# Seven-product pairs of the FFN up-projection in groups of two with one ordinary pair between, and their fourth weight sum made by VectorE instead of an adding DMA

## The reference, cut to what matters

```python
D_FF = 2816
def conv_ffn(x, w_up, conv_w, conv_b, w_down):
    h = x @ w_up                       # (512, 1024) @ (1024, 5632)
    ch = h.shape[-1]
    h = lax.conv_general_dilated(h, conv_w[:, None, :], window_strides=(1,), padding=((CONV_WIDTH - 1, 0),), ...,
                                 feature_group_count=ch) + conv_b
    gate, val = jnp.split(h, 2, axis=-1)
    return (jax.nn.silu(gate) * val) @ w_down
```

## Time and profile before

| | us |
|---|---|
| median of three runs | 2041.09 |
| the profiled execution's own time | 2042.29 |
| its span, first to last instruction | 2040.6 |
| PE busy | 2026.4 (99%) |
| DVE (VectorE) busy | 1619.3 (79%) |
| ACT (ScalarE) busy | 1115.0 (55%) |
| POOL (GpSimd) busy | 433.7 (21%) |

### The profile page before, as it was taken

One profiled execution on the slowest core, in us unless ns is written; L12 is line 12 of the kernel. 1 busy time (PEld: TensorE's weight loads), 2 busy tenths in 40 slices (PEclk: granted clock), 3 DMA queues, 4 the chain that ended last, 5 costly groups with the idle time before them and its releaser, 6 DMA issues.

```text
span 2040.6 us, 33333 instructions
## 1 busy us (share of the span) xinstructions
PE 2026.4 (99%) x12636; PEld 1750.7 (86%) x12636; DVE 1619.3 (79%) x2555; ACT 1115.0 (55%) x1861; POOL 433.7 (21%) x482
## 2 busy tenths in 40 slices
PE   9999999999999999999999999999999999999998
PEld 8889998888988899888877888998888889999887
DVE  6668878889467887899888669777997668877898
ACT  4755545447335555546656646555465755545555
POOL 0520332210000232120035402322110520332220
PEclk9999999999999999999999999999999999999999
DMA  8123344384432334467421123334674122334393
GB/s 291 64 104 125 109 130 150 121 255 172 145 129 75 97 105 129 145 190 243 166 73 42 63 83 104 119 104 155 197 237 163 65 104 83 109 122 147 115 269 122
DMA packets 82570, 276.42 MB, mean 135 GB/s; under 512 B 9408, under 2 KB 13632, under 8 KB 82032
## 3 DMA queue, kind: packets, MB, share of 16 engines
q1 hardware_dynamic: 59184, 214.67, 30.4%
q0 software_dynamic: 11200, 24.12, 5.8%
q10 hardware_dynamic: 12032, 35.54, 4.8%
HBM read 256.43 MB, written 14.73 MB: 133 GB/s over the span
## 4 chain that ended last, share of the span: by engine, by line
PE 91%; DVE 5%; DMA 2%; ACT 1%; issue 0%; DVEq 0%; ACTq 0%; SPq 0%
PE ps L2437 12%; PE ps L2438 12%; PE ps L2439 12%; PE ps L2649 6%; PE ps L3018 5%; PE ps L3019 5%; PE ps L3020 5%; PE ps L2976 5%; PE ps L2978 5%; PE ps L2977 5%; PE ps L2509 2%; PE ps L2465 2%; PE ps L2466 2%; PE ps L2467 2%; DMA raw<-slabs 2%; PE ps L2497 1%
## 5 line engine op out<-in xcount | busy, mean ns | idle before, releaser
L2437 PE MATMUL ps<-h_hi,w_hi 128*128 128x512 f32 (+1 forms) x1104 | 433.0, 392 | 0.0
L2438 PE MATMUL ps<-h_lo,w_hi 128*128 128x512 f32 (+1 forms) x1104 | 429.6, 389 | 0.0
L2439 PE MATMUL ps<-h_hi,w_lo 128*128 128x512 f32 (+1 forms) x1104 | 428.9, 389 | 0.0
L1603 DVE TENSOR_TENSOR w_lo<-raw,w_hi 128x1024 fp32r<-128x1024 f32 x300 | 372.0, 1247 | 39.1 <-ACT w_hi L901 35.5
L901 ACT ACTIVATE w_hi<-raw 128x1024 fp32r<-128x1024 f32 x312 | 326.4, 1053 | 133.1 <-DVE raw L2251 74.0
L2437 PEld LDWEIGHTS ps<-h_hi,w_hi 128*128 128x128 f32 x1104 | 207.6, 188 | 44.0 <-issue 4.0
L2439 PEld LDWEIGHTS ps<-h_hi,w_lo 128*128 128x128 f32 x1104 | 207.3, 188 | 43.2
L2438 PEld LDWEIGHTS ps<-h_lo,w_hi 128*128 128x128 f32 x1104 | 207.7, 188 | 38.9
L1281 ACT ACTIVATE work<-ps,conv_sb 128x512 f32<-128x512 f32 x120 | 93.0, 775 | 162.6 <-PE ps L2439 133.2
L3018 PE MATMUL ps<-w_hi,h_hi 128*128 128x512 f32 x408 | 159.7, 391 | 2.1 <-DVE w_lo L1603 2.1
L3020 PE MATMUL ps<-w_hi,h_lo 128*128 128x512 f32 x408 | 158.8, 389 | 0.0
(11 more groups left out here) (365 smaller groups left out, 5054.6 us busy)
## 6 DMA issues: line engine op xcount, KB each, us to landing
raw<-slabs SPq DMA_DIRECT2D x368, 512.0 KB, 4.1
act<-slabs POOLq DMA_DIRECT2D x64, 256.0 KB, 5.6
bias<-slabs SPq DMA_DIRECT2D x16, 512.0 KB, 6.3
x_dram<-x ACTq DMA_DIRECT2D x16, 512.0 KB, 5.0
x<-x_dram ACTq DMA_DIRECT2D x16, 512.0 KB, 4.9
raw<-act POOLq DMA_DIRECT2D x28, 256.0 KB, 3.3
act<-slabs SPq DMA_DIRECT2D x12, 512.0 KB, 5.4
bias_dram<-bias_rows ACTq DMA_DIRECT2D x2, 2048.0 KB, 12.3
```

What stands on the lines that cost most here:

```text
L1603: ve.tensor_tensor(w_lo[:, c % RING, :], raw[:, raw_slot(c), :], w_hi[:, c % RING, :].bitcast(f32), ALU.subtract).then_inc(lo_made, 1)
L2437: pe.matmul(ps[:, bank, cols], hi, h_hi[:, k, cols], start=k == 0, stop=False)
L2438: pe.matmul(ps[:, bank, cols], hi, h_lo[:, k, cols], start=False, stop=False)
L2439: last = pe.matmul(ps[:, bank, cols], lo, h_hi[:, k, cols], start=False, stop=k == KT - 1)
```

## The change

The seven-product pairs become 4, 6, 7, 9, 10, 12, 13, 15 and 16, nine in a layer in place of seven. Pair 4 with pair 5 keeps a queue of its own (`first_period`), and four groups follow, of two seven-product pairs f and g = f + 1 and one ordinary pair n = f + 2 (f = 6, 9, 12, 15). PSUM's eight banks go round in fours of two for all pairs of this stretch. In a group TensorE runs p1, p2, p6, p5, p7 of f, p1 and p2 of g, p4 and p3 of f, p6, p5, p7 of g, the first slab of n, p4 and p3 of g, the second slab of n. The fourth weight sum is made by VectorE (`x4`) and the adding DMA is gone. SP's loads stand in the order of the pairs. Both engines' queues are written anew. Cut to its core:

```diff
-FASTS = (FAST_END - FAST) // 2
+GROUPS_OF_THREE = 6, 9, 12, 15
+FAST_PAIRS = [FAST] + [q + e for q in GROUPS_OF_THREE for e in range(2)]
+FASTS = len(FAST_PAIRS)
+X1_ORDER = [FAST] + [q + e for q in GROUPS_OF_THREE for e in (1, 0)]
+UP_PRODUCTS = [(FAST, p) for p in (1, 2, 6, 4, 3)] + [
+    (q + e, p) for q in GROUPS_OF_THREE
+    for e, p in ((0, 1), (0, 2), (0, 6), (1, 1), (1, 2), (0, 4), (0, 3), (1, 6), (1, 4), (1, 3))]
...
-            return (0 if q // 2 % 2 else 4) + e
+            return 2 * ((q + 2) % 4 if FAST <= q < FAST_END else q % 2) + e
...
-                for q in range(FAST, FAST_END + 2, 2):
+                for q in range(FAST, FAST_END + 1):
                     for e in range(2):
                         c = up_slab(L, q, e)
-                        if q == FAST:
+                        if q - 2 not in FAST_PAIRS:
                             sp.wait_ge(lo_made, made(c - RAW))
                         elif e:
-                            sp.wait_ge(part_lo_made["x3"], fast(L, q - 2) + 1)
-                            sp.wait_ge(part_lo_made["x4"], fast(L, q - 2) + 1)
+                            sp.wait_ge(part_lo_made["x3"], part_count(L, q - 2, "x3"))
+                            sp.wait_ge(part_lo_made["x4"], part_count(L, q - 2, "x4"))
                         else:
-                            sp.wait_ge(part_lo_made["x1"], fast(L, q - 2) + 1)
+                            sp.wait_ge(part_lo_made["x1"], part_count(L, q - 2, "x1"))
                             sp.wait_ge(up_x2, fast(L, q - 2) + 1)
                             sp.wait_ge(up_x3, fast(L, q - 2) + 1)
                         sp.dma_start(raw[:, raw_slot(c), :], slabs[dram(c)]).then_inc(raw_in[raw_slot(c)], 16)
-                    if q < FAST_END:
-                        for e in range(2):
-                            c = up_slab(L, q + 1, e)
-                            sp.wait_ge(lo_made, made(c - RAW))
-                            sp.dma_start(raw[:, raw_slot(c), :], slabs[dram(c)]).then_inc(raw_in[raw_slot(c)], 16)
...
-            def fourth_sum(L, q):
-                pool.wait_ge(up_x2, fast(L, q) + 1)
-                pool.wait_ge(part_lo_made["a11"], fast(L, q) + 1)
-                pool.dma_start(raw[:, raw_slot(up_slab(L, q, 1)), SEQ:D], sum_place(), accum_op=ALU.add)\
-                    .then_inc(up_x4, 16)
...
-                fourth_sum(L, FAST)
                 for j in range(STEPS - 1):
                     down_sums(L, j)
-                    if FAST <= 2 * j + 4 < FAST_END and j:
-                        fourth_sum(L, 2 * j + 4)
...
+                def period(f):
+                    g, n = f + 1, f + 2
+                    more = n + 1 < FAST_END
+                    slab_tap(f - 1, 1)
+                    part_hi(f, "x3")
+                    copy(f, 0)
+                    part_hi(g, "a11")
+                    slab_silu(f - 1)
+                    copy(f, 1)
+                    part_hi(f, "x4")
+                    copy(f, 2)
+                    part_hi(g, "x2")
+                    copy(g, 0)
+                    part_hi(g, "x3")
+                    slab_tap(f, 0)
+                    split_hi(up_slab(L, n))
+                    slab_tap(f, 1)
+                    copy(g, 1)
+                    slab_silu(f)
+                    split_hi(up_slab(L, n, 1))
+                    part_hi(g, "x4")
+                    copy(g, 2)
+                    if more:
+                        part_hi(f + 4, "x1")
+                        slab_tap(g, 0)
+                        part_hi(f + 3, "a11")
+                        part_hi(f + 3, "x2")
+                        slab_tap(g, 1)
+                        part_hi(f + 3, "x1")
                     else:
                         sc.dma_start(x[:, 0, :], x_dram[0]).then_inc(x_back, 16)
                         sc.dma_start(x[:, 1, :], x_dram[1]).then_inc(x_back, 16)
                         operand(L, 0)
                         for j in range(4):
                             s1(L, j)
-                        fast_tap(q, 0)
+                        slab_tap(g, 0)
                         sc.dma_start(x[:, 2, :], x_dram[2]).then_inc(x_back, 16)
                         sc.dma_start(x[:, 3, :], x_dram[3]).then_inc(x_back, 16)
-                        sc.wait_ge(up_mm, 5 * fast(L, q) + 5)
-                        split_hi(up_slab(L, q + 2))
-                        fast_tap(q, 1)
-                        split_hi(up_slab(L, q + 2, 1))
-                    silu(0, i)
-                    tap(1, i, 0)
+                        split_hi(up_slab(L, n + 1))
+                        slab_tap(g, 1)
+                        split_hi(up_slab(L, n + 1, 1))
+                    slab_tap(n, 0)
+                    slab_silu(g)
...
+                def x4(q):
+                    row1 = raw_slot(up_slab(L, q, 1))
+                    ve.wait_ge(up_x2, fast(L, q) + 1)
+                    ve.wait_ge(part_lo_made["a11"], part_count(L, q, "a11"))
+                    ve.tensor_tensor(raw[:, row1, SEQ:D], raw[:, row1, SEQ:D], sum_place(), ALU.add).then_inc(up_x4, 1)
...
                 def x2(q):
@@ -2084,7 +2147,8 @@
                     ve.wait_ge(raw_in[row1], raw_count(up_slab(L, q, 1)))
                     if q > FAST:
                         ve.wait_ge(part_lo_made["x2"], fast(L, q))
-                        ve.wait_ge(up_x4, 16 * fast(L, q))
+                        ve.wait_ge(up_x3, fast(L, q))
+                        ve.wait_ge(up_x4, fast(L, q))
...
+                def first_period(q):
                     slab_taps(q - 1, 1)
-                    if q > FAST:
-                        part_lo(q, "x3")
                     split_lo(up_slab(L, q + 1))
-                    gate(1, i - 1)
+                    slab_gate(q - 1)
                     split_lo(up_slab(L, q + 1, 1))
                     c11(q)
                     part_lo(q, "x4")
                     c22(q)
-                    if q + 2 < FAST_END:
-                        x1(q + 2)
-                        x2(q + 2)
-                        part_lo(q + 2, "a11")
-                        part_lo(q + 2, "x2")
-                        slab_taps(q, 0)
-                        c12(q)
-                        part_lo(q + 2, "x1")
-                        slab_taps(q, 1)
-                        x3(q + 2)
+                    x1(q + 2)
+                    x2(q + 2)
+                    x1(q + 3)
+                    part_lo(q + 2, "a11")
+                    part_lo(q + 2, "x2")
+                    slab_taps(q, 0)
+                    c12(q)
+                    part_lo(q + 3, "x1")
+                    part_lo(q + 2, "x1")
+                    slab_taps(q, 1)
+                    x3(q + 2)
+                    slab_gate(q)
+                    x4(q + 2)
...
+                def period(f):
+                    g, n = f + 1, f + 2
+                    more = n + 1 < FAST_END
+                    slab_tap(f - 1, 0, 1)
+                    if f > GROUPS_OF_THREE[0]:
+                        part_lo(f, "x1")
+                    slab_tap(f - 1, 1, 1)
+                    slab_tap(f - 1, 0, 0)
+                    part_lo(f, "x3")
+                    slab_tap(f - 1, 1, 0)
+                    part_lo(g, "a11")
+                    slab_gate(f - 1)
+                    x2(g)
+                    c11(f)
+                    c22(f)
+                    part_lo(f, "x4")
+                    part_lo(g, "x2")
+                    x3(g)
+                    part_lo(g, "x3")
+                    x4(g)
+                    slab_tap(f, 0, 1)
+                    c12(f)
+                    slab_tap(f, 0, 0)
+                    split_lo(up_slab(L, n))
+                    slab_tap(f, 1, 1)
+                    c11(g)
+                    slab_tap(f, 1, 0)
+                    split_lo(up_slab(L, n, 1))
+                    slab_gate(f)
+                    c22(g)
+                    part_lo(g, "x4")
+                    if more:
+                        x1(f + 3)
+                        x1(f + 4)
+                        part_lo(f + 4, "x1")
+                        x2(f + 3)
+                        c12(g)
+                        slab_tap(g, 0, 1)
+                        part_lo(f + 3, "a11")
+                        slab_tap(g, 1, 1)
+                        slab_tap(g, 0, 0)
+                        part_lo(f + 3, "x2")
+                        slab_tap(g, 1, 0)
+                        x3(f + 3)
+                        slab_gate(g)
+                        x4(f + 3)
                     else:
                         operand(L, 0)
                         for j in range(4):
                             s1(L, j)
-                        slab_taps(q, 0)
-                        c12(q)
-                        split_lo(up_slab(L, q + 2))
-                        slab_taps(q, 1)
-                        split_lo(up_slab(L, q + 2, 1))
-                    gate(0, i)
-                    slab_taps(q + 1, 0)
+                        c12(g)
```

(107 more changed lines are left out.)

78 lines of the change are left out of this document (45 added, 33 removed).

## The result

The changed kernel takes 2080.47 us (median, 2077.99 to 2082.92), the kernel before 2040.65 measured beside it: a ratio of 1.0196, 95% interval 1.0183 to 1.0209, or 39.8 us slower. The forecast was 34.8 us slower, 2075.9.

What follows compares the result with a forecast made beforehand. VectorE's queue and the second load carry the loop; per layer 1.23 (first group) + 3 x 3.00 (steps) - 1.52 (TensorE's saving) = 8.71, four layers 34.8: 2075.9 us, range 2060 to 2092.

Steps and rivals of the forecast that it cites:

- The loop of 34.12: VectorE's queue from x1(f+4) to the next one, closed through the second load: 34.12 us against TensorE's 31.12, 3.00 lost per step.
- a): Loop part: x1 until seen, ScalarE's x1 hi and two handovers, 1.80 us.
- b): Loop part on VectorE: x1 lo and x2(f+3), 1.74 us.
- c): Loop part on VectorE: c12(g), four taps of g, a11 lo, x2 lo, x3, gate and x4, 6.75 us.
- d): Loop part on VectorE, next period: x1 lo, four taps of the ordinary pair, x3 lo, a11 lo, 5.76 us.
- e): Loop part on VectorE from gate and x2 until x4 lo is seen, with 0.76 idle for x3 hi: 13.05 us.
- f): Loop part: the second load's issue behind x4 lo, its landing at 4.5 and x1's start, 5.02 us.
- The first group: First group of each layer: load issue, new x4 and VectorE's queue make p1(7) 1.23 us late.
- TensorE's waits: In a group TensorE waits some 2 us before p5(f) for x1 lo, some 0.9 more before p7(f) for ScalarE's copy.
- The last group: Last group of a layer: no x1 behind it, so TensorE runs through without idle.
- both that leave the load out: Rivals: TensorE stays the bound, loads in time, 2035.0 us, chance 0.06; second load hidden, 2038.1 us, chance 0.05.
- the hidden load: Rival: second load hidden, only VectorE's order binds, groups of 31.30 us: 2038.1 us, no measurable change, chance 0.05.

Runs made afterwards that it cites:

- e9: Changed kernel with the fourth sum by adding DMA, as in e8, and the load order of e1: 2035.24 us, ratio 0.9967 to the kernel before.
- e4: Kernel before, alternating pairs kept, with the fourth sum alone moved from the adding DMA to VectorE: 2042.86 us, ratio 1.0005.
- e8: Changed kernel with the fourth sum by adding DMA again, each DMA ahead of GpSimd's sums that gate late: 2066.17 us, ratio 1.0121.
- e2: Changed kernel with the even slab of pair f+4 loaded behind the odd slab of f+4, third in its burst: 2107.84 us, ratio 1.0321.
- e1: Changed kernel with SP loading the even slab of pair f+4 ahead of the odd slab of f+3: 2038.95 us, ratio 0.9988.
- e6: Changed kernel with e1's load order and the fourth sum by adding DMA, GpSimd's sums ahead of the DMA: 2087.23 us, ratio 1.0232.
- e10: Changed kernel, loads unmoved, with x1(f+4) and its lo moved back in VectorE's queue, its hi in ScalarE's: 2065.38 us, ratio 1.0119.
- e3: Changed kernel with the fourth sum made by the adding DMA again, its issues laid between GpSimd's sums: 2083.40 us, ratio 1.0210.

## Why the prediction was right

- **TensorE is the bound and spared 1.52 us per layer**: right. e9 shows it undisturbed: the stretch of the first layer is 145.43 long, against 147.11.
- **The loop of 34.12**: right, 34.33 from 254.81 to 289.14. By its parts: a) 1.82 (1.80 was forecast), b) 1.75 (1.74), c) 6.50 (6.75), d) 5.80 (5.76), e) 13.39 (13.05), f) 5.07 (5.02). Part c) is shorter since taps from different slabs stand 0.66 apart and not 0.72; e) is longer since x4 lo takes 1.11 beside GpSimd's sums, where I had put 0 for GpSimd. The two errors nearly cancel, and that is luck. One reading was off: of the 18 such landings in the first three layers of the kernel before, six and not five take 5.0 us or more, and their mean is 4.65; with it the forecast would have been 2.4 us higher. Here the load took 4.6 from its issue to its landing (284.52 to 289.11).
- **The first group**: right in three layers. In layer 1 it is 32.43 us (31.12 + 1.23 forecast). In layer 0 it is 35.68, and this is the term that was too small. Its x1(7) began 16.7 us after p1(4), 1.5 later than in the other layers (15.2), as the load came 6.4 after SP's issues began at 214.05. Then p6(6) waited 1.92, where it waits 0.47 in layer 1, and 16 of the matmuls behind it came 0.21 apart in place of 0.12: 1.5 us more. In layer 3 one load was waited for 5.47 instead of some 4.4: 1.0 us. Layer 0 is 3.5 us longer than layer 1, and layer 3 is 1.2 longer; these are most of the 5.0 us by which the forecast was short.
- **TensorE's waits**: the step failed as to their place. I had 2 us before p5 and 0.9 before p7. The trace of a steady group has idle time before p6 as well, 0.91, then 0.37 before p5 and 0.60 before p7:

```profile
264.75 0.39 PE L3098 MATMUL ps<-work_r,a_hi 128*128 128x256 f32 x1 [0.91 <-ACT bias L1318]
266.81 0.39 PE L3098 MATMUL ps<-g_post_r,w_hi 128*128 128x256 f32 x1 [0.37 <-DVE w_lo L2120]
269.11 0.36 PE L3098 MATMUL ps<-x_r,a_hi 128*128 128x256 f32 x1 [0.60 <-ACT bias L1318]
```

  What I missed: `copy(f, 0)`, for which p6 waits, stands behind x3 hi in ScalarE's queue, and x3 is made late on VectorE. The amounts fit better than the places: set against the same group of e9, start by start, TensorE is 1.15 us late at p6, 1.77 at p5 (2 were forecast), 2.63 at p7 (0.9 more, as forecast), 2.98 at p1(g) and 3.04 from p2(g) to the end of the group. The sum, 3.00 a group, did not depend on the place.
- **VectorE's wait of over 4 us before x1(f+4)**: right, twelve waits of 3.96 to 5.47, one for each step from group to group, 53.2 us together. The four x1(7) of the first groups wait 2.13, 0.53, 0.50 and 0.51. **The last group**: I said that it has no wait; no x1 follows in it, but its window is 34.12 like the others, since it takes over the lateness of its own p1(g). The forecast's sum had counted that.
- **The adding DMA's removal at no cost or gain, in the idle time**: right for the kernel before (e4), incomplete for the groups: there two x4 of 0.60 are in the loop, and without them the kernel is 14.3 us faster (e8).
- **The rivals**: both that leave the load out are refuted by the result and by e2, and e1 turns the changed kernel into nearly what they describe: 2038.95, where the hidden load was priced at 2038.1. The Trainium skill's rule of occupancy (Perfetto Trace Analysis, Identifying the Most-Contended Engine) would have named TensorE in both kernels, 99% and 98%: the trace agrees as to the name, and the loss is in none of the two shares.

## What to carry to other kernels

Where queues are written by hand, close the loop: from a waiting instruction through everything behind it in its queue to the event that lets the awaited load go, then the load, and compare the sum with what the bounding engine needs. VectorE's busy share says little, 89% as reckoned for a group and 92% as measured in e1; the same work ran at 31.1 or at 34.1 us a group by the order of two loads. Let a load whose place is already free go ahead of one that still waits for its place, and look at each queue for what stands behind the wait.

## What the runs showed that I had not expected

The granted clock after a wait. Behind the 1.92 us before p6(6) of the changed kernel, and behind 2.91 in e2 and 4.04 in e6, it fell to the lower level, 1.2 GHz; behind waits of 0.91 and of 0.60 in the later groups, and behind 1.40 in e10, it stayed at 2.4 GHz. The windows of the first layer:

```profile
228.00:230.00 2.00, 0.08 (x1) 0.00 (x0) 2.00 (x4) 0.95 (x3) 0.00 (x0) 1.00 0.00 0
230.00:232.00 2.00, 2.00 (x11) 2.00 (x12) 2.00 (x4) 0.90 (x1) 0.00 (x0) 0.61 0.77 252
232.00:234.00 2.00, 2.00 (x12) 2.00 (x12) 2.00 (x4) 0.90 (x2) 0.00 (x0) 0.54 0.03 10
234.00:236.00 2.00, 2.00 (x19) 2.00 (x18) 2.00 (x4) 0.63 (x1) 0.74 (x1) 1.00 0.00 0
```

By the starts of the matmuls, TensorE is 2.08 us late at p6(6) and 3.66 behind p5(6): a stall of 2.1 us so cost 3.7. And GpSimd's sums can hold a VectorE subtraction for 2.9 us (e3), three times the 0.92 that I had set as the most for one set of sums.
